# A gated feed-forward product in a two-block Trainium2 kernel: a plain product replaced by Strassen's 2x2 block scheme

## The reference, cut to what matters

```
D_MODEL = 1024; SEQ = 1024; D_FF = 2816
...
h = rmsnorm(x, g_ffn_pre[l])
f = (jax.nn.silu(h @ w_gate[l]) * (h @ w_up[l])) @ w_down[l]
x = x + rmsnorm(f, g_ffn_post[l])
```

## Time and profile before

| | before |
|---|---|
| runs shown (us) | 5148.79, 5151.25, 5138.72; median 5148.79 |
| profiled execution, own time | 5145.13 us |
| its span | 5143.3 us |
| mean granted TensorE clock | 0.973 |
| PE busy | 4834.0 us (94%) |
| DVE busy | 2188.9 us (43%) |
| ACT busy | 1408.6 us (27%) |
| POOL busy | 949.4 us (18%) |
| the `Gemm` stage | first matmul at 1024.40, first matmul of the next stage at 1632.38 us |

### The profile page before, as it was taken

One profiled execution on the slowest core, in us unless ns is written; L12 is line 12 of the kernel. 1 busy time (PEld: TensorE's weight loads), 2 busy tenths in 40 slices (PEclk: granted clock), 3 DMA queues, 4 the chain that ended last, 5 costly groups with the idle time before them and its releaser, 6 DMA issues. The chain is left out here.

```text
span 5143.3 us, 96674 instructions
## 1 busy us (share of the span) xinstructions
PE 4834.0 (94%) x41758; PEld 3016.4 (59%) x41758; DVE 2188.9 (43%) x3870; ACT 1408.6 (27%) x2411; POOL 949.4 (18%) x1108
## 2 busy tenths in 40 slices
PE   7999888999999999999899988899999989999988
PEld 4444865444444444555599965564454489985663
DVE  3780537400000112763244556555385244536644
ACT  1220344100000101322133335453232123226542
POOL 0010411000000000000133324450010033224460
PEclk8999999999999999999999999999999999999999
DMA  3443012311112542433421111312254332111022
GB/s 122 160 153 118 2 54 84 98 33 41 35 39 86 173 170 92 157 138 129 137 59 52 46 39 52 89 42 86 99 180 155 104 109 59 46 41 59 28 73 94
DMA packets 334282, 454.35 MB, mean 88 GB/s; under 512 B 37112, under 2 KB 262424, under 8 KB 332913
## 3 DMA queue, kind: packets, MB, share of 16 engines
q1 hardware_dynamic: 288480, 273.59, 17.0%
q0 software_dynamic: 45392, 174.74, 9.6%
HBM read 324.73 MB, written 137.11 MB: 90 GB/s over the span
## 5 line engine op out<-in xcount | busy, mean ns | idle before, releaser
L483 PE MATMUL psum<-arena 128*128 128x512 f32 (+1 forms) x3424 | 1355.6, 555 | 12.2 <-POOLq L222 9.2
L483 PEld LDWEIGHTS psum<-arena 128*128 128x128 f32 x3424 | 650.0, 191 | 688.5 <-issue 656.4
L2621 PE MATMUL psum<-arena 64*64 64x64 f32 (+5 forms) x23040 | 908.3, 232 | 35.1 <-DMA arena<-rw_Q 23.9
L2621 PEld LDWEIGHTS psum<-arena 64*64 64x64 f32 (+3 forms) x23040 | 868.7, 144 | 76.2 <-issue 48.2
L768 PE MATMUL psum<-arena 128*128 128x512 f32 x1536 | 664.0, 593 | 10.5 <-DVEq L222 6.1
L349 PE MATMUL psum<-arena 128*128 128x512 f32 x1408 | 607.1, 594 | 3.3 <-POOLq L222 3.3
L768 PEld LDWEIGHTS psum<-arena 128*128 128x128 f32 x1536 | 289.9, 190 | 369.9 <-issue 361.5
L349 PEld LDWEIGHTS psum<-arena 128*128 128x128 f32 x1408 | 267.0, 190 | 343.0 <-issue 343.0
L2044 DVE CUSTOM_DVE_ANT_0 arena<-psum,arena 128x512 f32<-128x512 f32 (+3 forms) x532 | 292.9, 589 | 323.9 <-PE psum L1931 305.8
L1931 PE MATMUL psum<-arena 64*128 64x512 f32 (+3 forms) x1192 | 274.8, 547 | 103.4 <-DVE arena L2044 67.2
L2009 ACT COPY arena<-psum 128x512 f32<-128x512 f32 (+3 forms) x532 | 244.6, 512 | 307.5 <-PE psum L1982 301.3
(11 more groups left out here) (316 smaller groups left out, 4323.1 us busy)
## 6 DMA issues: line engine op xcount, KB each, us to landing
arena<-w_down SPq DMA_DIRECT2D x88, 512.0 KB, 3.5
arena<-w_in SPq DMA_DIRECT2D x86, 512.0 KB, 4.5
proj<-arena SPq DMA_DIRECT2D x42, 640.0 KB, 5.5
arena<-w_mod POOLq DMA_DIRECT2D x24, 1024.0 KB, 6.2
proj<-arena SPq DMA_DIRECT2D x44, 512.0 KB, 5.2
arena<-proj POOLq DMA_DIRECT2D x34, 640.0 KB, 5.0
arena<-proj SPq DMA_DIRECT2D x28, 640.0 KB, 7.1
x_home<-arena POOLq DMA_DIRECT2D x26, 512.0 KB, 3.0
```

The costliest lines, as they stand in the source:

```text
L483: ins = pe.matmul(self.c.psum[:, g % 3, 0:n1 - n0], self.unit(i)[:, k, :], self.moving(k, n0, n1), start=(k == 0), stop=(k == KT - 1))
L2621: return pe.matmul(out, lhsT, rhs, start=first, stop=last, skip_group_check=not (first and last))
```

## The change: one stage written anew

`Gemm` is replaced by `GatedPairs`. It works on 256 feed-forward columns of one weight matrix at a time: 11 pairs of tiles, first gate and then up, so 22 units. A unit is a product of a 2x2 block matrix A (weights: first index the tile of the pair, second the half of K) with a 2x2 block matrix B (activations: first index the half of K, second the half of the tokens). The plain way takes eight block products of four matmuls each; the scheme takes seven, P1 to P7, from sums of blocks: S1 = A21+A22, S2 = S1-A11, S3 = A11-A21, S4 = A12-S2, T1 = B12-B11, T2 = B22-T1, T3 = B22-B12, T4 = B21-T2. VectorE makes the T once, ahead of unit 0, and the four S for each unit, one unit ahead. P1 and P2 share bank 0, P5 and P3 bank 1, P6, P7 and P4 bank 2; the even and the odd units have three banks each. P1 is copied out by ScalarE before P2 is added onto it; VectorE adds what a bank holds to the kept blocks at five points of a unit. The other sums are made in the banks, where one product is accumulated onto another. In odd (up) units VectorE multiplies each finished block with the Silu that ScalarE made of the gate unit.

With this go four smaller things. The loads are 1 MB each, in pieces of 1 KB instead of 512 B, into three slots of 2048 columns. The first of them waits for the sixth weight row of the stage ahead, no longer for the eighth. Slots 6 and 7 of `core.W` now hold the gate blocks, so the seventh `w_down` load waits for the stage's meeting (`after={6: ffn.meet}`). There is no hardware loop any more.

```diff
--- before.py
+++ after.py
@@ -260,161 +260,169 @@
                 stage.leave(meets)
-class Gemm(Stage):
...
+class GatedPairs(Stage):
+    ORDER = (("P1", 0, "A11", "B11"), ("P5", 1, "S1", "T1"), ("P6", 2, "S2", "T2"), ("P2", 0, "A12", "B21"),
+             ("P7", 2, "S3", "T3"), ("P3", 1, "S4", "B22"), ("P4", 2, "A22", "T4"))
+    def __init__(self, core, room, w_gate, w_up, x, out):
         super().__init__(core)
...
+        self.w, self.out, half = (w_gate, w_up), out, KT // 2
+        self.N = 2 * (FFT // 2)
+        self.B = {f"B{i + 1}{j + 1}": x[:, half * i:half * i + half, 512 * j:512 * j + 512] for i in range(2) for j in range(2)}
+        for t in ("T1", "T2", "T4"):
+            self.B[t] = room.take(core, half, 512)
+        self.B["T3"] = self.B["B12"]
+        self.S = [{s: room.take(core, half, P) for s in ("S1", "S2", "S4")} for _ in range(2)]
+        self.g = [[core.W[:, 6144 + 512 * (2 * i + j):6144 + 512 * (2 * i + j) + 512] for j in range(2)] for i in range(2)]
+        self.y = {(0, 0): None, **{ij: room.take(core, 512) for ij in ((0, 1), (1, 0), (1, 1))}}
+        self.free = max(core.unit_used[0:6])
+        pe, act, dve = [], [], [f"{x}{i}" for i in (1, 2, 3, 4) for x in ("S0_", "T")]
+        for u in range(self.N):
+            pe += [f"{p}_{u}" for p, _, _, _ in self.ORDER]
+            act += [f"c{u}"] + ([] if u % 2 else [f"g{u}_{ij}" for ij in ("11", "22", "12", "21")])
+            dve += [f"p5_{u}", f"u2_{u}"] + ([f"S{u + 1}_4"] if u + 1 < self.N else []) + ([f"m{u}_11"] if u % 2 else [])
+            for ij in ("22", "12", "21"):
+                dve += [f"c{u}_{ij}"] + ([f"m{u}_{ij}"] if u % 2 else [])
+        self.s_pe, self.s_act, self.s_dve = Steps(core.pe, pe, 1), Steps(core.act, act, 1), Steps(core.dve, dve, 1)
+        self.in_base = [core.w_in[i].planned for i in range(3)]
+        for u in range(self.N):
+            core.w_in[u % 3].planned += 16
+            for i in range(2):
+                core.unit_used[2 * (u % 3) + i] = self.s_pe.at(0, f"P4_{u}")
+        core.unit_used[6] = core.unit_used[7] = 0
+    def unit(self, u):
+        return self.c.W[:, u % 3 * 2048:u % 3 * 2048 + 2048].rearrange("p (k f) -> p k f", k=KT)
+    def left(self, u, name):
+        if name in self.S[0]:
+            return self.S[u % 2][name]
+        i, j = {"A11": (0, 0), "A12": (0, 1), "A21": (1, 0), "A22": (1, 1), "S3": (1, 0)}[name]
+        return self.unit(u)[:, KT // 2 * j:KT // 2 * j + KT // 2, P * i:P * i + P]
+    def bank(self, u, b):
+        return self.c.psum[:, 3 * (u % 2) + b, :]
+    def kept(self, u, i, j):
+        return self.y[i, j] if u % 2 else self.g[i][j]
+    def wait_weights(self, eng, u):
+        eng.wait_ge(self.c.w_in[u % 3].sem, self.in_base[u % 3] + 16 * (u // 3 + 1))
     def sp(self, sp):
...
+        E = self.s_pe
+        if self.free:
+            sp.wait_ge(E.sem, self.free)
+        for u in range(self.N):
+            if u >= 3:
+                sp.wait_ge(E.sem, E.at(0, f"P4_{u - 3}"))
+            col = u // 2 * (2 * P)
+            sp.dma_start(self.unit(u), self.w[u % 2][:, :, col:col + 2 * P]).then_inc(self.c.w_in[u % 3].sem, 16)
     def run_pe(self, pe):
...
+        E, A, Dv = self.s_pe, self.s_act, self.s_dve
+        for u in range(self.N):
+            self.wait_weights(pe, u)
+            for p, b, left, right in self.ORDER:
+                if p == "P1" and u >= 2:
+                    empty = Dv if u % 2 else A
+                    pe.wait_ge(empty.sem, empty.at(0, f"{'m' if u % 2 else 'g'}{u - 2}_11"))
+                if p in ("P5", "P6") and u >= 2:
+                    pe.wait_ge(Dv.sem, Dv.at(0, f"c{u - 2}_{'12' if p == 'P5' else '21'}"))
+                if left[0] == "S":
+                    pe.wait_ge(Dv.sem, Dv.at(0, f"S0_{left[1]}" if u == 0 else f"S{u}_4"))
+                if u == 0 and right[0] == "T":
+                    pe.wait_ge(Dv.sem, Dv.at(0, right))
+                if p == "P2":
+                    pe.wait_ge(A.sem, A.at(0, f"c{u}"))
+                for first, taken in (("P7", f"u2_{u}"), ("P3", f"p5_{u}"), ("P4", f"c{u}_22")):
+                    if p == first:
+                        pe.wait_ge(Dv.sem, Dv.at(0, taken))
+                L, R = self.left(u, left), self.B[right]
+                begins, ends = p in ("P1", "P5", "P6"), p in ("P2", "P3", "P4")
+                for k in range(KT // 2):
+                    ins = pe.matmul(self.bank(u, b), L[:, k, :], R[:, k, :], start=(begins and k == 0),
+                                    stop=(k == KT // 2 - 1), skip_group_check=True)
+                ins.then_inc(E.sem, 1)
     def run_act(self, act):
...
+        E, A, Dv = self.s_pe, self.s_act, self.s_dve
+        for u in range(self.N):
+            act.wait_ge(E.sem, E.at(0, f"P1_{u}"))
+            if u >= 2:
+                act.wait_ge(Dv.sem, Dv.at(0, f"m{u - 1 - u % 2}_21"))
+            act.copy(self.kept(u, 1, 0), self.bank(u, 0)).then_inc(A.sem, 1)
+            if u % 2 == 0:
+                act.wait_ge(E.sem, E.at(0, f"P2_{u}"))
+                if u >= 2:
+                    act.wait_ge(Dv.sem, Dv.at(0, f"m{u - 1}_11"))
+                act.activation(self.g[0][0], self.bank(u, 0), ACT.Silu).then_inc(A.sem, 1)
+                for i, j in ((1, 1), (0, 1), (1, 0)):
+                    act.wait_ge(Dv.sem, Dv.at(0, f"c{u}_{i + 1}{j + 1}"))
+                    act.activation(self.g[i][j], self.g[i][j], ACT.Silu).then_inc(A.sem, 1)
     def run_dve(self, dve):
...
+        E, A, Dv, B = self.s_pe, self.s_act, self.s_dve, self.B
+        def left_sums(u, first):
+            L = lambda name: self.left(u, name)
+            for i, (dst, a, b, op) in enumerate((("S1", "A21", "A22", ALU.add), ("S2", "S1", "A11", ALU.subtract),
+                                                 ("S3", "A11", "A21", ALU.subtract), ("S4", "A12", "S2", ALU.subtract))):
+                if i in (1, 3):
+                    dve.drain()
+                ins = dve.tensor_tensor(L(dst), L(a), L(b), op)
+                if first:
+                    ins.then_inc(Dv.sem, 1)
+                    t, x, y = (("T1", "B12", "B11"), ("T2", "B22", "T1"), ("T3", "B22", "B12"), ("T4", "B21", "T2"))[i]
+                    if i in (1, 3):
+                        dve.drain()
+                    dve.tensor_tensor(B[t], B[x], B[y], ALU.subtract).then_inc(Dv.sem, 1)
+            if not first:
+                ins.then_inc(Dv.sem, 1)
+        self.wait_weights(dve, 0)
+        left_sums(0, True)
+        for u in range(self.N):
+            b0, b1, b2 = [self.bank(u, b) for b in range(3)]
+            y = lambda i, j: self.kept(u, i, j)
+            def times(i, j, x):
+                dve.wait_ge(A.sem, A.at(0, f"g{u - 1}_{i + 1}{j + 1}"))
+                dve.tensor_tensor(self.out[:, u - 1 + i, 512 * j:512 * j + 512], x, self.g[i][j], ALU.mult).then_inc(Dv.sem, 1)
+            dve.wait_ge(E.sem, E.at(0, f"P5_{u}"))
+            dve.wait_ge(A.sem, A.at(0, f"c{u}"))
+            if u >= 2:
+                dve.wait_ge(Dv.sem, Dv.at(0, f"m{u - 1 - u % 2}_21"))
+            dve.tensor_tensor(y(1, 1), b1, y(1, 0), ALU.add).then_inc(Dv.sem, 1)
+            dve.wait_ge(E.sem, E.at(0, f"P6_{u}"))
+            dve.tensor_tensor(y(0, 1), b2, y(1, 0), ALU.add).then_inc(Dv.sem, 1)
+            if u + 1 < self.N:
+                self.wait_weights(dve, u + 1)
+                if u >= 1:
+                    dve.wait_ge(E.sem, E.at(0, f"P4_{u - 1}"))
+                left_sums(u + 1, False)
+            if u % 2:
+                dve.wait_ge(E.sem, E.at(0, f"P2_{u}"))
+                times(0, 0, b0)
+            for i, j, bank, done, part in ((1, 1, b2, "P7", "p5"), (0, 1, b1, "P3", "u2"), (1, 0, b2, "P4", None)):
+                dve.wait_ge(E.sem, E.at(0, f"{done}_{u}"))
+                if part:
+                    dve.wait_ge(Dv.sem, Dv.at(0, f"{part}_{u}"))
+                dve.tensor_tensor(y(i, j), y(i, j), bank, ALU.add).then_inc(Dv.sem, 1)
+                if u % 2:
+                    dve.wait_ge(Dv.sem, Dv.at(0, f"c{u}_{i + 1}{j + 1}"))
+                    times(i, j, y(i, j))
 class Proj(Stage):
@@ -3353,13 +3361,13 @@
         TokenGemm(core, Room((big, TOP)), [token(a["w_out"], k) for k in range(KT)], lambda k, t: mixT[:, k, t * P:(t + 1) * P],
                   tiles, "rms", {"g": row_of(a["rows"], 0)}, hT, again=True, after={0: gdn.meet})
         act = R(big, FFT, SEQ)
-        Gemm(core, [kview(a["w_gate"]), kview(a["w_up"])], [(0, 0, KT), (1, 0, KT)], [(0, FFT, 0)],
-             lambda k, n0, n1: hT[:, k, n0:n1], two, "gated", 4, R(big, FFT * SEQ), R(big + FFT * SEQ, 2, 512)).close()
+        room = Room((big + FFT * SEQ, TOP), (h_at + KT * SEQ, h_at + KT * TOK2))
+        ffn = GatedPairs(core, room, kview(a["w_gate"]), kview(a["w_up"]), hT, act)
         scale, shift = [[lambda k, i=i, c=c: ms[:, 0, i * KT + k, c:c + 1] for c in range(2)] for i in (1, 0)]
```

(2 more changed lines are left out.)

126 lines of the change are left out of this document (removed).

## The result

| | before | after |
|---|---|---|
| median of the runs (us) | 5148.78 (5138.72 to 5151.25, 4 runs) | 5076.93 (5064.58 to 5078.74, 4 runs) |
| ratio, 95% interval | | 0.9859 [0.9838, 0.988] |
| profiled execution: own time, span | 5145.13, 5143.3 | 5075.14, 5073.4 |
| first matmul of the stage to the first of the next | 607.98 | 534.51 |

The kernel is 1.4% faster, 71.9 us in the medians and 69.9 in the two profiled spans. The forecast was 5074. The interval of the ratio stands for 62 to 83 us. Two later series of the same changed kernel gave medians of 5070.8 and 5082.7 us beside 5149.6 and 5148.1 of before, so a single median is good to some 6 us.

The account below looks back on a forecast made before the run. TensorE's matmuls were taken to bound the stage. The terms -75.5 - 1.9 + 2.9 + 1.7 = -72.8 us gave 5072.3 from the profiled execution and 5076.0 from the median, so 5074 us; own range 5062 to 5087, with rivals 5062 to 5091.

Parts of the forecast that it names:

- The matmuls: In the replaced stage, 704 matmuls become 616, or 1408 records become 1232 of the same shape: 75.5 us less.
- The new work within a unit: Copies, sums and S of VectorE and ScalarE in each unit stay hidden by the matmuls: 0 us.
- The 2.6 us to spare: Within a unit, the tightest answers to TensorE were counted ready 2.6 us before they are needed.
- The T: Ahead of unit 0, VectorE makes the T in time for the products: 0 us, at worst 2.5 us.
- The loads at the start: Weight loads issued earlier let the x_home store land before VectorE's last instruction, so the first matmul comes 1.9 us earlier.
- The end: Ahead of the next stage, TensorE waits about 3.7 us for the first w_down load instead of 0.83: +2.9 us.
- The clock behind it: Behind the gap ahead of the next stage, the clock falls to 0.50: +1.7 us, bounds 0 and 3.2.
- A cost at each product start: Rival: each of 154 product starts costs 0.1 us, 15.4 us in all, so 5089 us; chance 8%.
- A starved next stage: Rival: the next stage's first group also waits for the second or third weight row, 6 us, so 5080; chance 5%.
- The slower rival: VectorE's sum of P1 and P6 comes too late for P7 in every unit: 101 us more, 5175 us; chance 3%.
- The 3.3 us at which all of the gain should be gone: Stall of TensorE per unit, short of losing the clock, that would eat the whole gain: 72.8/22 = 3.3 us.

Follow-up runs that it names:

- Experiment 2: The changed kernel with P1's four matmuls run twice in each unit, so eight groups of four instead of seven: 5144.02 us, ratio to before 0.9993.
- experiment 3: The changed kernel with P2 moved right behind P1, then P5, P6, P7, P3, P4: 5127.30 us.
- experiment 5: The changed kernel with the first weight load waiting for the eighth weight row again, not the sixth: 5066.98 us in a single execution.
- experiment 4: The changed kernel with 5, 9 or 11 extra VectorE additions per unit ahead of the sum with bank 1: 5075.98, 5121.13, 5167.22 us.

## Why the prediction was right, step by step

**The matmuls** (forecast -75.5): the busy time fell by 607.1 - 530.9 = 76.2 us. 75.5 are the 176 records; the other 0.7 goes with less time at the low clock at the start (21 records took 11.89 us before, 19 take 9.98 now). Experiment 2 shows that nothing else carries the gain in the stage.

**The new work within a unit** (forecast 0): no wait inside the stage. The 2.6 us to spare were right: five extra additions cost nothing outside unit 0, and nine gave the pause that the schedule says, 1.50 us. It is the order P1, P5, P6, P2 that hides it (experiment 3).

**The T** (forecast 0): a T took 2.29 us, less than the 2.45 counted, and no product of unit 0 waited. It is the thinnest place: with five extra additions, 3.8 us, unit 0 alone waited, 1.9 us, so it had 1.9 us to spare and not the 2.5 (14.4 to 16.9) of the forecast.

**The loads at the start** (forecast -1.9): the wait ahead of the stage fell from 3.25 to 1.26 us, -2.0. The mechanism was the one given, and of its two parts it is the earlier issue (experiment 5).

**The end** (forecast +2.9): 3.60 instead of 0.83, +2.8, released by the w_down load.

**The clock behind it** (forecast +1.7): 39 records took 18.67 us where 39 x 0.4289 + 0.16 = 16.89 would do, +1.8. The size is right, but the sum counts in full what is only likely (its bound of 0 allowed for that). Ahead of the next stage the clock was lost in all eight profiles with a gap of 3.52 to 3.9 us, and not after the 3.50 us of experiment 5. Of the 21 pauses of 3.02 to 3.38 us in experiment 4 six lost it, and of the pauses up to 1.84 us in the stage (experiments 3 and 4) none. What decides between equal pauses is not shown. The Trainium skill ("TensorE: Matmul & The Clock Gate", "Why this matters for your kernels") asks for no idle gaps above about 3 us. In these runs that is where losses begin, not an edge.

The terms sum to -76.2 - 2.0 + 2.8 + 1.8 = -73.6 us, and the span fell by 69.9. The 3.7 us between lie in stages that were not changed. The largest piece is in the second block, the same 1663 records before and after:

```profile
4616.00:4828.40 212.40, 189.15 (x1663) 0.97 0.15 52
```

```profile
4541.00:4759.60 218.60, 194.97 (x1663) 0.94 0.15 51
```

There the changed kernel takes 6.2 us more, 5.8 of it in busy matmuls at a lower mean clock; other stretches give some back. The prediction had no term for this, and the rows of before give none: unchanged stages have more time at the low clock in one run than in another. So a part of how close 5074 came to 5076.9 is luck; the two later series lie 3 below and 9 above the forecast.

**The rivals.** A cost at each product start did not show (pitch unchanged over 154 starts). A starved next stage did not show: one wait, on the first row. The slower rival did not happen, and experiment 4 made it happen: with the sum 3.04 us late in the units the kernel is 0.35% slower than before. The time was close (5175 us forecast for pauses of 2.95, 5167 measured at 3.04), but by two errors that partly cancel: each break costs 0.25 us besides the pause, which I left out, and the clock is lost in some pauses, not in all, which I counted in full. The 3.3 us at which all of the gain should be gone was too high for the same reasons: between the medians with nine and eleven additions, the kernel before is met at a pause of about 2.5 us (an estimate, by a straight line from 5121 at 1.50 to 5167 at 3.04).

## What to carry to other kernels

Where TensorE is fed without gaps, a scheme with fewer products pays its whole count, as long as the elementwise answers have a product or two between them and the matmuls that need them; count that cover in microseconds from the row of one addition, and choose the order of the products by it. Look at the two ends of a rewritten stage by themselves: which slot is freed last decides when the next stage's first load may start, and a transfer issued a few microseconds earlier may clear the way for a store that opens the stage. A pause of TensorE counts with its break, and from about 3 us on with a chance of the clock behind it.

## What the runs showed of the hardware that was not expected

- A pause of TensorE costs 0.25 us besides its length (44 pauses, 11.1 us more busy time; 22 pauses, 5.9 us).
- Equally long pauses of 3.04 us lose the clock or keep it. Where one lost it, the clock was low in two stretches of 2 us (0.58 and 0.56) and then back at 1.00, and the records behind it took 1.7 us longer.
- Whole runs of one program differ by 6 to 27 us, and stretches without any change differ with the mean granted clock (0.97 and 0.94 above).
- A 512 KB store took 2.9 us alone, 3.5 to 4.6 behind weight loads that were nearly done, and 5.8 and 6.5 in the midst of them.
